# The recurrent stage's matrix inverses: the squarings of four chunks on one 128x128 block diagonal instead of two 64x64 ones

## What is computed

```
def step(state, inp):
    r_t, w_t, k_t, v_t, a_t, b_t = inp
    sa = jnp.einsum('bhvk,bhk->bhv', state, a_t)
    state = state * w_t[:, :, None, :] + sa[..., None] * b_t[:, :, None, :] + v_t[..., None] * k_t[:, :, None, :]
    return state, jnp.einsum('bhvk,bhk->bhv', state, r_t)
```

## Time and profile before

| | |
|---|---|
| median of 3 runs | 2790.38 us (2789.25 to 2798.33) |
| the profiled execution | 2792.68 us |
| its span in the trace | 2790.8 us |
| mean granted TensorE clock | 0.965 |
| TensorE matmul busy | 2551.2 us (91%) |
| VectorE, ScalarE busy | 1210.2 us (43%), 770.8 us (28%) |
| the groups of the recurrent stage | 1358 to 1586 us of the span |

### The profile page before, as it was taken

One profiled execution on the slowest core, in us unless ns is written; L12 is line 12 of the kernel. 1 busy time (PEld: TensorE's weight loads), 2 busy tenths in 40 slices (PEclk: granted clock), 3 DMA queues, 4 the chain that ended last, 5 costly groups with the idle time before them and its releaser, 6 DMA issues. The chain is left out here.

```text
span 2790.8 us, 48901 instructions
## 1 busy us (share of the span) xinstructions
PE 2551.2 (91%) x21256; PEld 1797.2 (64%) x21256; DVE 1210.2 (43%) x2020; ACT 770.8 (28%) x1267; POOL 59.7 (2%) x52
## 2 busy tenths in 40 slices
PE   8998889899999999899899979979898998889887
PEld 7998667799999988677677757643333333333232
DVE  7764666544466652566544458531111111111113
ACT  3221354442344431345233236321000000000001
POOL 1000022100000000000000000010000000000000
PEclk9999899999999999999999999989999999999999
DMA  5545441355322233433212112489999999999996
GB/s 160 143 127 120 94 164 58 127 190 167 115 92 91 91 100 116 146 114 125 82 56 103 43 73 107 154 340 430 431 431 430 430 431 431 430 431 431 430 430 273
DMA packets 142773, 609.68 MB, mean 218 GB/s; under 512 B 37536, under 2 KB 57120, under 8 KB 117536
## 3 DMA queue, kind: packets, MB, share of 16 engines
q1 hardware_dynamic: 113616, 571.15, 52.3%
q10 hardware_dynamic: 28944, 35.40, 3.9%
HBM read 566.68 MB, written 37.47 MB: 216 GB/s over the span
## 5 line engine op out<-in xcount | busy, mean ns | idle before, releaser
L3826 PE MATMUL moe_bank<-moe_ring,xg 128*64 128x512 f32 x2048 | 490.7, 623 | 87.9 <-DMA moe_ring<-in_w_exp_up 87.1
L3826 PEld LDWEIGHTS moe_bank<-moe_ring,xg 128*64 128x64 f32 x2048 | 155.1, 141 | 365.6 <-issue 356.8
L4111 DVE TENSOR_TENSOR moe_sg<-moe_sg,moe_bank 64x512 f32<-64x512 f32 x64 | 44.2, 690 | 576.8 <-ACT moe_sg L3978 576.8
L3855 PE MATMUL moe_bank<-moe_ring,moe_act_t 128*64 128x512 f32 x1008 | 227.0, 592 | 0.5 <-ACT moe_act_t L3985 0.5
L68 PE MATMUL ffn_prod<-ffn_x_low,ffn_w_high 128*128 128x258 f32 x704 | 200.1, 284 | 5.8 <-PEq L138 5.8
L69 PE MATMUL ffn_prod<-ffn_x_high,ffn_w_low 128*128 128x258 f32 x704 | 200.1, 284 | 0.0
L70 PE MATMUL ffn_prod<-ffn_x_high,ffn_w_high 128*128 128x258 f32 x704 | 199.3, 283 | 0.0
L68 PE MATMUL in_bank<-x_low,in_w_high 128*128 128x264 f32 x640 | 185.6, 290 | 14.5 <-DVE in_w_low L987 9.2
L70 PE MATMUL in_bank<-x_high,in_w_high 128*128 128x264 f32 x640 | 183.7, 287 | 0.0
L69 PE MATMUL in_bank<-x_high,in_w_low 128*128 128x264 f32 x640 | 183.3, 286 | 0.0
L3855 PEld LDWEIGHTS moe_bank<-moe_ring,moe_act_t 128*64 128x64 f32 x1008 | 72.2, 137 | 144.0 <-issue 143.4
(11 more groups left out here) (590 smaller groups left out, 5304.0 us busy)
## 6 DMA issues: line engine op xcount, KB each, us to landing
moe_ring<-in_w_exp_gate SPq DMA_DIRECT2D x64, 2048.0 KB, 27.6
moe_ring<-in_w_exp_up SPq DMA_DIRECT2D x64, 2048.0 KB, 21.3
moe_ring<-in_w_exp_down SPq DMA_DIRECT2D x63, 2048.0 KB, 25.8
ffn_w<-in_w_up SPq DMA_DIRECT2D x44, 512.0 KB, 4.3
in_w<-in_w_in SPq DMA_DIRECT2D x40, 512.0 KB, 4.0
front_w<-in_w_in SPq DMA_DIRECT2D x32, 512.0 KB, 3.5
ffn_w<-in_w_down SPq DMA_DIRECT2D x16, 704.0 KB, 4.1
rw_w<-in_w_in SPq DMA_DIRECT2D x18, 512.0 KB, 3.9
```

The costliest lines, as they stand in the source:

```text
L3826: last = nc.tensor.matmul(bank[64 * g:64 * g + 64, s], xe[:, (e // BATCH) % 2, k, at:at + CAPACITY], ring[:, slot_of(n, g), k * HALF:(k + ...
L3855: last = nc.tensor.matmul(bank[64 * h:64 * h + 64, 3 + e % 2], act_t[:, s, j], weights[:, at:at + HALF], start=(c == 0 and j == 0), stop=( ...
L4111: nc.vector.tensor_tensor(sg[0:CAPACITY, s], sg[0:CAPACITY, s], bank[64:64 + CAPACITY, s], ALU.mult).then_inc(act_ready, 1)
```

## The change

The four chunks' triangles now stand on one diagonal of 128x128: A and its transpose get four zeroed column blocks and one plain one, so 5 instead of 3 blocks each. One matmul on all 128 partitions takes the place of two on 64. ScalarE writes five copies in rounds 0 to 2 and four in round 3; VectorE's spread and masks write five blocks instead of three. `ch` loses its second buffer, and VectorE's spread of round 0 now waits for `first_inverse`, which reads the block that it overwrites. The constants `masks` and `eyes` grow accordingly. One step of side work moves from slot 1 (ahead of round 1) to slot 2 (between rounds 1 and 2).

```diff
-GROUP_STEPS = (1, 2, 2, 1, 1, 2, 1, 2, 1, 2)
+GROUP_STEPS = (1, 1, 3, 1, 1, 2, 1, 2, 1, 2)
...
-        masks = sb("masks", [P, 2, 9, RCHUNK])
-        eyes = sb("eyes", [P, HEAD_DIM + 4 * RCHUNK])
+        masks = sb("masks", [P, 2, 13, RCHUNK])
+        eyes = sb("eyes", [P, HEAD_DIM + 6 * RCHUNK])
...
-        ch = sb("ch", [P, 2, heads_all, 7 * RCHUNK])
+        ch = sb("ch", [P, heads_all, 11 * RCHUNK])
...
-                    for q in range(3 if l + 1 < LEVELS - 1 else 2):
-                        last = nc.scalar.activation(ch[:, (l + 1) % 2, :, q * RCHUNK:(q + 1) * RCHUNK], made, ACT.Copy,
+                    for q in range(5 if l + 1 < LEVELS - 1 else 4):
+                        last = nc.scalar.activation(ch[:, :, q * RCHUNK:(q + 1) * RCHUNK], made, ACT.Copy,
...
-                        for c in range(2):
-                            last = nc.tensor.matmul(bank[heads(c), CHAIN_BANK, at + first:at + upto], now[heads(c), n, A_BOTH],
-                                                    now[heads(c), n, AT_ONE.start + first:AT_ONE.start + upto], start=True, stop=True)
+                        last = nc.tensor.matmul(bank[:, CHAIN_BANK, at + first:at + upto], ch[:, n, A_ALL],
+                                                ch[:, n, AT_ONE.start + first:AT_ONE.start + upto], start=True, stop=True)
                         if l < LEVELS - 1:
-                            for c in range(2):
-                                last = nc.tensor.matmul(bank[heads(c), CHAIN_BANK + 1, n * RCHUNK:(n + 1) * RCHUNK],
-                                                        now[heads(c), n, AT_BOTH], now[heads(c), n, A_ONE], start=True, stop=True)
+                            last = nc.tensor.matmul(bank[:, CHAIN_BANK + 1, n * RCHUNK:(n + 1) * RCHUNK], ch[:, n, AT_ALL],
+                                                    ch[:, n, A_ONE], start=True, stop=True)
...
-                        first = ch[:, 0, e::2, 0:6 * RCHUNK].rearrange("p x (a q f) -> p x a q f", a=2, q=3)
+                        first = ch[:, e::2, 0:10 * RCHUNK].rearrange("p x (a q f) -> p x a q f", a=2, q=5)
...
                     if l < LEVELS - 2:
-                        three = [P, heads_all, 3, RCHUNK]
-                        nc.vector.tensor_tensor(ch[:, (l + 1) % 2, :, AT_PLACE].rearrange("p n (q f) -> p n q f", q=3),
-                                                made[..., AT].unsqueeze(2).broadcast_to(three),
-                                                sides.unsqueeze(1).broadcast_to(three), ALU.mult).then_inc(inverse_ready, 1)
+                        spread = [P, heads_all, 5, RCHUNK]
+                        if l == 0:
+                            dve.wait_ge(inverse_ready, INVERSES[-1] * g + 1)
+                        nc.vector.tensor_tensor(ch[:, :, AT_PLACE].rearrange("p n (q f) -> p n q f", q=5),
+                                                made[..., AT].unsqueeze(2).broadcast_to(spread),
+                                                sides.unsqueeze(1).broadcast_to(spread), ALU.mult).then_inc(inverse_ready, 1)
```

More of the change, by code:

```diff
@@ L2728, in rwkv7 @@
         eye_chunk = eyes[:, HEAD_DIM:HEAD_DIM + RCHUNK]
-        sides = eyes[:, HEAD_DIM + RCHUNK:].rearrange("p (q f) -> p q f", q=3)
+        sides = eyes[:, HEAD_DIM + RCHUNK:].rearrange("p (q f) -> p q f", q=5)
         first_states = states[:].rearrange("p a n k -> p (a n k)")
@@ L2741, in rwkv7 @@
         AT, PT = (slice(n * RCHUNK, (n + 1) * RCHUNK) for n in range(2))
-        A_BOTH, A_ONE = slice(0, 2 * RCHUNK), slice(2 * RCHUNK, 3 * RCHUNK)
-        AT_BOTH, AT_PLACE = slice(3 * RCHUNK, 5 * RCHUNK), slice(3 * RCHUNK, 6 * RCHUNK)
-        AT_ONE, P_PLACE = slice(5 * RCHUNK, 6 * RCHUNK), slice(6 * RCHUNK, 7 * RCHUNK)
+        A_ALL, A_ONE = slice(0, P), slice(P, P + RCHUNK)
+        AT_ALL, AT_PLACE = slice(5 * RCHUNK, 5 * RCHUNK + P), slice(5 * RCHUNK, 10 * RCHUNK)
+        AT_ONE, P_PLACE = slice(9 * RCHUNK, 10 * RCHUNK), slice(10 * RCHUNK, 11 * RCHUNK)
         B_TOK, K_TOK, V_TOK = (slice(n * FIELD, n * FIELD + HEAD_DIM) for n in range(3))
@@ L3080, in chain_round @@
                 def chain_round(g, l):
-                    now = ch[:, l % 2]
                     if l == 0:
@@ L3282, in mask @@
                             [P, RW_X, 3, RCHUNK]), ALU.mult).then_inc(masked, 1)
-                        first = ch[:, 0, e::2, 0:6 * RCHUNK].rearrange("p x (a q f) -> p x a q f", a=2, q=3)
+                        first = ch[:, e::2, 0:10 * RCHUNK].rearrange("p x (a q f) -> p x a q f", a=2, q=5)
                         for a, n in ((0, 4), (1, 0)):
-                            nc.vector.tensor_tensor(first[:, :, a], made[:, :, n].unsqueeze(2).broadcast_to([P, RW_X, 3, RCHUNK]),
-                                                    masks[:, d, 3 * a + 3:3 * a + 6].unsqueeze(1).broadcast_to([P, RW_X, 3, RCHUNK]),
+                            nc.vector.tensor_tensor(first[:, :, a], made[:, :, n].unsqueeze(2).broadcast_to([P, RW_X, 5, RCHUNK]),
+                                                    masks[:, d, 5 * a + 3:5 * a + 8].unsqueeze(1).broadcast_to([P, RW_X, 5, RCHUNK]),
                                                     ALU.mult).then_inc(masked, 1)
@@ L3290, in first_inverse @@
                     dve.wait_ge(masked, 6 * (g + 1))
-                    nc.vector.tensor_tensor(ch[:, 1, :, P_PLACE], ch[:, 0, :, AT_ONE], eye_chunk.unsqueeze(1).broadcast_to(
+                    nc.vector.tensor_tensor(ch[:, :, P_PLACE], ch[:, :, AT_ONE], eye_chunk.unsqueeze(1).broadcast_to(
                         [P, heads_all, RCHUNK]), ALU.add).then_inc(inverse_ready, 1)
@@ L3309, in inverse @@
                     dve.wait_ge(inverse_ready, INVERSES[-1] * g + INVERSES[l])
-                    to = ch[:, (l + 1) % 2, :, P_PLACE] if l < LEVELS - 1 else inv[:]
-                    nc.vector.tensor_tensor(to, ch[:, l % 2, :, P_PLACE], made[..., PT], ALU.add).then_inc(inverse_ready, 1)
+                    to = ch[:, :, P_PLACE] if l < LEVELS - 1 else inv[:]
+                    nc.vector.tensor_tensor(to, ch[:, :, P_PLACE], made[..., PT], ALU.add).then_inc(inverse_ready, 1)
                 def read_ends(g):
@@ L4400, in laid_out @@
     d["rw_eyes"] = np.concatenate([np.tile(np.eye(n, dtype=f32), (P // n, 1)) for n in (HEAD_DIM, RCHUNK)] + [
-        np.repeat((n // RCHUNK % 2 == side).astype(f32)[:, None], RCHUNK, 1) for side in range(2)] + [
+        np.repeat((n // RCHUNK == side).astype(f32)[:, None], RCHUNK, 1) for side in range(4)] + [
         np.ones((P, RCHUNK), f32)], 1)
@@ L4408, in laid_out @@
     s, t = n[:, None] % RCHUNK, np.arange(RCHUNK)[None, :]
-    sides = [(n // RCHUNK % 2 == side)[:, None] for side in range(2)] + [np.ones((P, 1), bool)]
+    sides = [(n // RCHUNK == side)[:, None] for side in range(4)] + [np.ones((P, 1), bool)]
     d["rw_masks"] = np.stack([np.stack([a <= b, a < b, a <= b] + [(a > b) & side for side in sides] +
```

## The result

| | before | the change |
|---|---|---|
| median | 2792.22 us (2789.25 to 2798.33) | 2831.99 us (2829.21 to 2834.14) |
| ratio | | 1.0144 [1.0126, 1.0161] |
| span of the profiled execution | 2790.8 us | 2828.9 us |
| mean granted TensorE clock | 0.965 | 0.962 |

The change is 1.4% slower: 39.8 us by the medians, 38.1 by the two spans. The forecast was 2829.9 us. (The brackets behind a median are its lowest and highest run, those behind a ratio its 95% interval.)

A forecast was written before the change was run, and what follows sets the result against it. TensorE was taken to set the recurrent stage's pace, on the kernel's critical chain: +37.1 us for rounds and +2.4 for other engines gave +39.5 on 2792.68, less 2.3, so 2829.9 us; 8-in-10 range 2820 to 2852.

The forecast's parts named there:

- the likeliest case: Whole kernel: slower because unpaired 128x128 weight loads hold TensorE longer in each round; 2829.9 us, chance 0.74.
- The step of a 128x128 load: TensorE in the changed rounds: each matmul instruction with 128x128 fp32 weights takes 112 ns, bounds 107 to 114.
- The rounds: Recurrent stage on TensorE: +0.98 us for each of rounds 0 to 2, +1.04 round 3, +0.39 round 4; +34.9 us together.
- Copies, spread, masks: ScalarE and VectorE per round: five copies 1.73 us, spread 1.17 us, masks 0.65 us, mostly hidden behind side work.
- wait for a single buffer: Operand buffers: single buffers cost nothing, since writes already waited for the reading round; the one new wait is on ended work.
- Waits between rounds 1 and 2: TensorE ahead of round 2: -0.65, -0.3, +0.4, +0.3 us in second to fifth group; none with 512-column side tiles.
- the stage's mean of 0.94: Recurrent stage: granted clock taken to stay at 0.94, turning the rounds' +34.9 us at full clock into +37.1 us.
- The rival that named it: Recurrent stage: the clock falls oftener; two more half-clock stretches of 6.8 us each, +14 us, 2844 us; chance 0.12.
- the price per instruction: Rival on TensorE's rounds: 32 ns per instruction whatever the weights, so the change is faster, 2761.5 us; chance 0.04.
- the load as cheap as a pair: Rival on TensorE's rounds: a 128x128 load takes 63 ns like a 64x64 pair; 2787 us, no visible difference; chance 0.03.
- The longer copies: Rival between rounds: ScalarE's copies become the wait, 24 gaps losing 0.69 us each, +17 us, 2847 us; chance 0.07.
- The first group: Start of the stage: masks uncovered +0.8 us, constants' transfer +0.4 us, and +0.5 us for no rows behind round 2.

The follow-up runs named there:

- seven waits for the copies instead of four: The changed kernel with the old GROUP_STEPS, six side matmuls instead of nine between rounds 1 and 2: 2846.39 us, ratio 1.0196.
- a longer cover: More side work between rounds 1 and 2 of early groups: on the change 2822.52 us; on the kernel before, run twice, 2786.65 and 2788.55 us.

## Why the prediction was right, point by point

The sign, the size (2829.9 us against 2832.0) and the likeliest case came out, and so did the cause. That the number came out within 2 us is partly luck. The forecast was +39.5 us. Measured by the spans it was +38.1, made of +28.5 for the stage at full clock, +12.6 for the clock in it and -3.1 in the rest of the kernel. The forecast had 37.3, 2.2 and nothing for these. Two terms were wrong by about 9 and 10 us and cancelled, and the change run a second time stood 47.8 us above the kernel before.

- **The step of a 128x128 load**: 112 ns forecast, 108 measured. It was the heart of the argument, that the earlier trace rows show one and 128 streamed columns at one price. The runs with 64x64 and 128x64 weights, which get 36 and 38 of the 40 us back, show it to be nearly the whole cause. The 63 ns that the prediction read for a pair of 64x64 counts the step out of the round among the 24; from first to last start it is 58.
- **The rounds**: +34.9 us at full clock forecast. From the last side matmul ahead to the first instruction behind, a two-product round of a late group went from 0.33 + 1.37 + 0.15 us to 0.23 + 2.48 + 0.11, +0.97, and round 4 by +0.33: 32 and 8 of them are +33.7.
- **Copies, spread, masks**: 1.73, 1.17 and 0.65 us forecast; five copies in a row are recorded with 1.67, the other two medians with 1.16 and 0.65. In the run with pairs on the new layout they cost TensorE some 1.6 us of gaps. No wait for a single buffer is seen, but no run takes the single buffers apart from the copies.
- **Waits between rounds 1 and 2**: forecast -0.65, -0.3, +0.4 and +0.3 us in the second to fifth group. The gaps ahead of round 2 went from 2.78, 1.26, 0.58 and 0.36 to 2.27, 0.89, 0.89 and 0.66: -0.5, -0.4, +0.3 and +0.3. No wait between rounds 1 and 2 in late groups, as said.
- **The clock was mis-sized.** The step "at the stage's mean of 0.94 it is +37.1" gave it 2.2 us, as if the clock of before would hold. It was 12.6 in the first profile of the change and 24.8 in the second. The rival that named it asked for two more stretches and +14 us; with 25 us more at half clock that rival is very nearly what happened, beside the forecast and not instead of it. It should have been a term of the sum.
- **A relief was missed.** Without the clock the stage grew by 28.5 us and not by the rounds' 33.7 with the small waits. The "issue" time fell by 3.8 us. The change issues 864 matmul instructions and as many loads fewer, and TensorE uses them more slowly, which fits the reading of these stops above. Some 1.6 us is not assigned.
- **The other rivals**: the price per instruction and the load as cheap as a pair are refuted by the 108 ns. The longer copies did not become the wait.

The first group is a small miss beside these. The idle time until the constants land went from 5.20 to 6.21 us, +1.0 where 0.4 was forecast; from the first mask to round 0 it is 4.56 instead of 3.77 us, the +0.8 of the forecast. Neither is in the 41.2 us: they lie ahead of the rounds, which begin at 1358.2 as before because VectorE came to the stage's first wait 1.9 us earlier.

## What to carry to other kernels

Price a short fp32 matmul that brings its own weights by the columns of the weights (here 108 ns for each of its two instructions with 128 columns, 58 ns for two tiles of 64 side by side). A padded diagonal that doubles the columns nearly doubled the price, and its zeros are paid like data. When TensorE is the bound and its clock is near the full level, allow for the half-clock stretch that may follow a new wait and not only for its own length, and read two profiles before trusting the amount. Before splitting work into more and shorter instructions, look at the packets of the instruction queue and at the "issue" waits: they are a second limit beside the engine.

## What was not expected of the hardware

- Short waits ahead of a round 2 went with long stretches at half clock: nine of nine stretches of 10 us or more, in three profiles of the new form, begin 0.3 to 3.2 us after such a round had started behind 0.3 to 1.9 us of waiting. In the change the second group's 13.6 us at half clock began 2.3 us after its round 2 had started; on the old form it was 0.6 us after. The amount scatters: 50.2 and 74.5 us in two profiles of one kernel, 81.9 with seven waits for the copies instead of four, 20.0 with nearly all of them away. In the three profiles with a longer cover, on either form, no wait ahead of a round 2 is over 0.6 us, and no stretch at half clock stands between 1386 us and the end of the rounds; one of 17.1 us follows the rounds in one of them. The longer cover took the waits and these stretches away together; why one wait is followed by a stretch and another is not stays open.
- Instructions come in packets of 16 KB, at the closest 3.27 us apart, and a stop of TensorE marked "issue" ends 1.2 to 1.6 us after a packet (124 of 124). That the packets are TensorE's is inferred from their number; the queue that holds the instructions was not seen itself.
- Weights of 128x64 in two column halves load side by side, at 58 ns a pair.
